# Placing the sample rows' search and ranking in one stretch of VectorE's order, and storing their mask already repeated for 128 partitions

## The chip, the cores and the metric

The kernel runs on one core of a Trainium2 chip. The metric is the device time of one launch in microseconds, and its median over three runs before the change is 3454.47 us (3447.92 to 3465.7). The engines are named as in the profile: PE (TensorE, matrix products and transposes), DVE (VectorE), ACT (ScalarE), POOL (GpSimd) and SP (SyncE), which here does nothing but issue DMAs. Each engine executes its own instructions strictly in the order in which they were written for it.

## The reference: what is computed

One step of a two-layer decoder trunk over 2048 prompt rows and 8 x 4 sample rows, D = 1024. Layer 0 projects the normed rows to two mixers, a sparse attention (A) and a retention (B). For mixer A an indexer gives each row a score for each key, and only the 256 best keys take part in the softmax:

```
sc = where(vis, index_scores(iq, ik, iw), -inf)
_, sel = top_k(sc, 256)            # 256 of 2048 keys for a prompt row, of 2052 for a sample row
ok = sel <= tpos
out = softmax(q . k[sel] where ok) . v[sel]      # GQA, 8 heads over 2 key heads
```

A sample row has 2048 keys in a paged cache and 4 new ones, so 2052 scores. Layer 1 is a gated DeltaNet and is not touched.

## The kernel before

The program is five stages with a barrier between them: `layer0_project`, `layer0_mixers`, `layer0_samples`, `layer0_out_and_conv` and `layer1_delta`. The change touches the second and the third.

In `layer0_mixers` the 2048 prompt rows are 16 tiles of 128 rows. A tile f passes through turning (`turn_q`, `turn_k`, `turn_b`), the retention (`ret_scores`, `ret_mask`, `ret_out`, `ret_update`, `gn_mean`, `gn_square`), the indexer (`index` on PE, `relu` on ACT, `weigh` on DVE), `bounds`, a bisection of 24 steps for the score of rank 256 (`count` on DVE for even tiles, `signs`/`side`/`move` on ACT for odd ones), `rank` and `mask`, and then attention (`scores` on PE, `masked` on DVE, `maxima`, `exp`, `turn_p`, `copy_p`, `times_v`). Beside all this PE computes the second half of the input projection (`project`), two contraction blocks at a time with weights that SP brings into four buffers (`load_w`, 512 KB each), and each load waits until `project` has let its buffer go.

The order in which each engine takes these steps is a list that `mixers_order` makes: each step has a place number (100 for one tile's round), the steps are sorted by it, and each engine walks its own part of the list. Signals (semaphores) only make an engine wait; they never change its order.

The 32 sample rows are searched for their 256 best keys in the same stage, by the steps of `sample_steps`. `s_bounds` gives the interval, `s_count` is one bisection step (one pass of DVE over 32 x 2052 scores and two tiny instructions), 24 of them; `s_rank` resolves ties: a pass for the scores above the interval, one for those within it, a running sum over them (a scan), and three passes that turn it into a mask of 0 and -1e30 in `s_row`. Before the change `s_rank` is cut into four steps that stand at four places with other work between them; `s_store` then writes the mask to `mb_s` in DRAM. The ties lie in the buffer `signs`, and ACT's first use of `signs` for tile 3 waits for the mask.

In `layer0_samples` partition 32 i + 8 r + q of `mb` needs the mask of sample row 8 i + q, for head r of 4, so each mask row is needed four times. SP's list there begins with some thirty loads, `mb` among them, then `gng`, `zb` and `za`; ACT's first instruction of the stage waits for all loads of `zb` and `za`, and everything that ACT copies for PE comes behind it.

Of the kernel before, what the change touches and what calls it, by code (L numbers as in the profile page):

```python
# [16 lines left out]
BF = mybir.dt.bfloat16  # L17
# [6 lines left out]
P = 128  # L24
D = 1024
# [480 lines left out]
def sample_steps(add):  # L506
# [18 lines left out]
    for k in range(STEPS):  # L525
        add(-226 + 10.0 * k if k < 2 else -177 + 7.4 * (k - 2), "dve", "s_count", k)
    for k in range(4):
        add((-8, 13.5, 33.5, 53.5)[k], "dve", "s_rank", k)
    add(90, "sp", "s_store")
# [33 lines left out]
def layer0_mixers(nc, io, S, both):  # L563
    ctx = ExitStack()
    with ctx:
# [15 lines left out]
        overm, signs = sb("overm", [P, SEQ], BF), sb("signs_out", [P, SKEYS], BF)  # L581
# [335 lines left out]
        def _(act):  # L917
# [37 lines left out]
            def count_signs(s, k):  # L955
                W = (s + 1) * P
                if (s, k) == (3, 0):
                    act.wait_ge(S["s_mask_ready"], after(1))
# [109 lines left out]
        def _(dve):  # L1068
            link, fresh = link_in(dve, S["dve_link"])

            def weigh(f, c, j):
# [5 lines left out]
                if j == 0:  # L1077
                    if (f, c) == (4, 0):
                        dve.wait_ge(S["s_mask_stored"], after(16))
# [159 lines left out]
            def s_rank(k):  # L1239
                w = s_halves[:, STEPS - 3:STEPS - 2]  # L1240
                over, tie, more, need_s = above[0:SR, :], signs[0:SR, :], cgt[0:SR], need[0:SR]
                if k == 0:
                    link(dve.tensor_tensor(hi_c[0:SR], s_mid, w, ALU.add))
                    link(dve.tensor_tensor(lo_c[0:SR], s_mid, w, ALU.subtract))
                    link(dve.tensor_scalar(over, s_row, hi_c[0:SR], 0.0, ALU.is_gt, ALU.add, accum_out=more))
                    link(dve.tensor_scalar(need_s, more, -1.0, float(TOPK), ALU.mult, ALU.add))
                elif k == 1:
                    link(dve.scalar_tensor_tensor(tie, s_row, lo_c[0:SR], over, ALU.is_gt, ALU.subtract))
                elif k == 2:
                    link(dve.tensor_tensor_scan(s_row, tie, tie, 0.0, ALU.add, ALU.bypass))  # L1250
                else:
                    link(dve.scalar_tensor_tensor(tie, s_row, need_s, tie, ALU.is_le, ALU.mult))
                    link(dve.tensor_tensor(tie, tie, over, ALU.add))
                    dve.tensor_scalar(s_row, tie, BIG, -BIG, ALU.mult, ALU.add).then_inc(S["s_mask_ready"], 1)
# [3003 lines left out]
```

## Time and profile before

| | |
|---|---|
| median of 3 runs | 3454.47 us (3447.92 to 3465.7) |
| the profiled execution's own time | 3465.7 us |
| its span, first to last instruction | 3464.1 us, so 1.6 us lie around it |
| PE busy | 3156.4 us, 91% |
| DVE / ACT / POOL busy | 53% / 39% / 26% |
| mean granted clock of PE | 0.957 |
| `layer0_mixers` | from about 375 to 1701 us of the span |
| `layer0_samples` | from about 1702 to 1805 us |

Busy shares are means over stages that have different limits. What a moved instruction is worth is to be read from the stretch in which it stands: which engine waits there, for whom, and how long. In the rows below a time in brackets is how long an engine stood before an instruction, and behind the arrow stands who released it. Where a line says x8 and gives a duration, it is the merged run of that many instructions.

### The profile page before, as it was taken

Reading aid. Unit: us, or ns where it says so; the run is one execution under the profiler, and the core shown is the slowest. Engines: PE = TensorE matmul, PEld = TensorE weight load, DVE = VectorE, ACT = ScalarE, POOL = GpSimd, SP = SyncE. Lnnn points to the kernel's source line nnn. Section 1 sums busy time; section 2 is a strip of 40 time slices with the busy share of each in tenths; the row PEclk is TensorE's granted clock in tenths of the full one; section 3 lists DMA queues with packets and bytes.
Section 4 is the critical chain, followed back from the end, with each engine's and each line's share of the span. In section 5 each row is a group of like instructions: output and inputs, shape, how many; then the busy total and the mean of one; then the engine's idle time right before and its main releaser. Section 6 shows DMA issues by size and latency. Waiting matters only on the chain. (4 is left out here: it accounts for less than half of the span.)

```text
span 3464.1 us, 46915 instructions
## 1 busy us (share of the span) xinstructions
PE 3156.4 (91%) x15557; PEld 1725.7 (50%) x15557; DVE 1835.2 (53%) x3700; ACT 1366.0 (39%) x2790; POOL 907.6 (26%) x1776
## 2 busy tenths in 40 slices
PE   8998989989998989888669999999999969989998
PEld 4554444444444444444344444444444456656664
DVE  0000496678878888864231531522513857656663
ACT  2221115667676767676332121121121334443442
POOL 2332333322322221000000000000000467765771
PEclk9999999999999999999879999999999989998999
DMA  6666767555443433301257021121111242234211
GB/s 193 179 197 226 226 212 217 174 166 166 137 132 118 126 113 100 120 22 34 86 211 265 25 70 55 31 67 49 37 64 32 65 155 100 84 98 140 80 62 67
DMA packets 260396, 407.35 MB, mean 118 GB/s; under 512 B 47896, under 2 KB 131138, under 8 KB 258978
## 3 DMA queue, kind: packets, MB, share of 16 engines
q1 hardware_dynamic: 237636, 387.64, 34.5%
q0 software_dynamic: 4096, 8.40, 0.9%
q10 hardware_dynamic: 18432, 8.40, 0.9%
q8 instruction: 125, 2.05, 0.2%
q14 instruction: 107, 0.87, 0.1%
HBM read 324.25 MB, written 103.03 MB: 123 GB/s over the span
## 5 line engine op out<-in xcount | busy, mean ns | idle before, releaser
L2576 PE MATMUL QB<-hT,w_c 128*128 128x512 f32 x1024 | 449.3, 593 | 0.0
L814 PE MATMUL PB<-wb,hT_ahead 128*128 128x512 f32 x832 | 417.2, 628 | 10.5 <-PEq L4165 4.6
L2576 PEld LDWEIGHTS QB<-hT,w_c 128*128 128x128 f32 x1024 | 190.1, 190 | 217.6 <-issue 217.6
L358 PE MATMUL P0A<-w_all,hT 128*128 128x512 f32 (+1 forms) x816 | 269.5, 490 | 2.4 <-issue 2.4
L1007 ACT COPY ptT<-PT 128x512 f32<-128x512 f32 (+3 forms) x320 | 164.0, 519 | 248.1 <-PE PT L825 247.7
L2427 PE MATMUL QA<-arena,hT 128*128 128x512 f32 (+1 forms) x768 | 255.1, 487 | 6.3 <-issue 3.0
L3628 PE MATMUL RPJ<-w_co,oT 128*128 128x512 f32 x544 | 250.0, 609 | 4.2 <-ACT oT L3796 3.2
L963 ACT ACTIVATE signs_out<-isc,mid 128x512 bf16<-128x512 f32 (+6 forms) x168 | 229.5, 1366 | 26.6 <-DVE mid L1107 25.5
L1119 DVE TENSOR_SCALAR_CACHE_REDUCE band<-isc,mid 128x384 bf16<-128x384 f32 (+6 forms) x168 | 236.4, 1407 | 1.3
L814 PEld LDWEIGHTS PB<-wb,hT_ahead 128*128 128x128 f32 x832 | 149.3, 198 | 169.0 <-issue 154.0
L3206 POOL TENSOR_SCALAR stat<-stat 128x1 f32<-128x1 f32 x16 | 3.1, 192 | 814.8 <-POOLq L122 814.8
L802 PE MATMUL PS<-kT,qT 64*128 64x512 f32 (+3 forms) x544 | 155.2, 595 | 57.4 <-DVE mxc L1167 57.0
L825 PE MATMUL PT<-ident,sm 128*128 128x128 f32 x1088 | 179.6, 285 | 30.6 <-ACT sm L997 25.4
L4122 POOL TENSOR_TENSOR arena<-arena 128x60 f32<-128x60 f32 (+24 forms) x465 | 167.2, 360 | 125.8 <-DVE arena L3975 91.7
L825 PEld LDWEIGHTS PT<-ident,sm 128*128 128x128 f32 x1088 | 122.6, 142 | 154.5 <-issue 85.1
L358 PEld LDWEIGHTS P0A<-w_all,hT 128*128 128x128 f32 x816 | 133.7, 192 | 127.0 <-issue 126.8
L2427 PEld LDWEIGHTS QA<-arena,hT 128*128 128x128 f32 x768 | 128.2, 193 | 130.6 <-issue 130.6
L2792 ACT COPY raw<-QB 128x512 f32<-128x512 f32 x64 | 37.5, 586 | 393.2 <-PE QB L2576 393.2
L1167 DVE CUSTOM_DVE_ANT_0 sm<-PS,mb 128x512 f32<-128x512 f32 (+3 forms) x272 | 153.9, 603 | 58.4 <-PE PS L802 58.2
L4125 POOL TENSOR_TENSOR arena<-arena 128x60 f32<-128x60 f32 (+24 forms) x465 | 167.8, 361 | 36.4
L997 ACT ACTIVATE sm<-sm,negm 128x128 f32<-128x128 f32 (+15 forms) x128 | 152.5, 1192 | 56.0 <-DVE negm L1179 27.9
L841 PE MATMUL PO<-ptT,vst 128*64 128x128 f32 x2176 | 155.6, 282 | 17.9 <-ACT ptT L1007 17.9
(541 smaller groups left out, 5332.5 us busy)
## 6 DMA issues: line engine op xcount, KB each, us to landing
wb<-in_w_in_ab SPq DMA_DIRECT2D x272, 512.0 KB, 3.8
out_c_all<-crow SPq DMA_DIRECT2D x256, 64.0 KB, 1.7
pra<-out_pr_all SPq DMA_DIRECT2D x16, 546.0 KB, 4.6
x_rows<-in_x_all SPq DMA_DIRECT2D x17, 512.0 KB, 5.8
out_hT_all<-hT SPq DMA_DIRECT2D x17, 512.0 KB, 3.1
arena<-out_c_all SPq DMA_DIRECT2D x17, 512.0 KB, 5.1
arena<-out_gc_rows SPq DMA_DIRECT2D x17, 512.0 KB, 3.7
cv<-out_c_all SPq DMA_DIRECT2D x17, 512.0 KB, 5.0
```

What stands on the lines that cost most here:

```text
L358: ins = pe.matmul(PA[u % 6][:, 0:b - a], hT[:, t % 3, c, :], w_all[:, c, a:b], start=(c == 0), stop=(c == KD - 1))
L814: ins = pe.matmul(b_bank(g, n)[:, :], h_of(g)[:, 2 * q + k, :], wb[:, u % 4, k, :], start=(q == 0 and k == 0), stop=(q == 3 and k == 1))
L825: ins = pe.transpose(PT[v % 2][:, k * P:(k + 1) * P], sm[:, 2 * (r % 2) + a, c * CH + k * P:c * CH + (k + 1) * P], ident[:, :])
L841: ins = pe.matmul(PO[a * HD:(a + 1) * HD, r * P:(r + 1) * P], vst[:, 4 * c + k, a * HD:(a + 1) * HD], ptT[:, (v + a) % 4, k * P:(k + 1) * ...
L963: act.activation(signs[:, 0:W], isc[:, s % 3, 0:W], ACT.Sign, bias=mid[:, s % 3:s % 3 + 1], scale=1.0, accum_out=cnt[:, s % 3:s % 3 + 1]). ...
L1007: act.copy(ptT[:, v % 4, 0:w], PT[v % 2][:, 0:w]).then_inc(S["p_copied"], 1)
L1119: link(dve.tensor_scalar(band[:, 0:W], isc[:, k, 0:W], m, 0.0, ALU.is_gt, ALU.add, accum_out=above_it))
L2427: ins = pe.matmul(PA[n % 2][:, 0:b - a], h, w_z[:, c, a:b], start=(c == 0), stop=(c == KD - 1))
L2576: ins = pe.matmul(PB[b % 2][:, 0:N], w_c[:, c, b * P:(b + 1) * P], hT[:, c, 0:N], start=(c == 0), stop=(c == KD - 1))
L3628: ins = pe.matmul(PJ[:, :], oT[:, c, :], w_co[:, c, n * 512:(n + 1) * 512], start=(c == 0), stop=(c == KD - 1))
L4122: link(pool.tensor_tensor(xtmp[:, 0:cl, 0:n], T[:, t % 2, j + 1:SB, j].unsqueeze(1).to_broadcast([P, cl, n]), Xs[:, t % 2, 0:cl, j:j + 1]. ...
L4125: ins = pool.tensor_tensor(Xs[:, t % 2, 0:cl, j + 1:SB], Xs[:, t % 2, 0:cl, j + 1:SB], xtmp[:, 0:cl, 0:n], ALU.subtract)
```

## The change

Five things are changed.

1. The 24 `s_count` steps stand at even distances (every 9.0 places from -226) rather than two at -226 and -216 and the rest every 7.4 places from -177.
2. `s_rank` is one step at place -8 rather than four at -8, 13.5, 33.5 and 53.5. It computes the same instructions in the same order. Its ties lie in `band` rather than in `signs`, which shrinks by four elements, and the wait for the mask moves from ACT (tile 3's first `signs`) to DVE (tile 2's first `count`, behind `s_rank` on the same engine).
3. `s_store` becomes four steps at 71, 75, 79 and 83 rather than one at 90, each of which issues four DMAs of 8 rows: 16 DMAs of 64 KB that write each mask row four times, and `mb_s` has 128 rows.
4. The first `weigh` of tile 4, which overwrites the scores, waits for all 16.
5. `layer0_samples` loads `mb` with one DMA of 128 rows rather than four that each repeat 8 rows four times.

```diff
     for k in range(STEPS):
-        add(-226 + 10.0 * k if k < 2 else -177 + 7.4 * (k - 2), "dve", "s_count", k)
-    for k in range(4):
-        add((-8, 13.5, 33.5, 53.5)[k], "dve", "s_rank", k)
-    add(90, "sp", "s_store")
+        add(-226 + 9.0 * k, "dve", "s_count", k)
+    add(-8, "dve", "s_rank")
+    for i in range(HB):
+        add(71 + 4 * i, "sp", "s_store", i)
...
-                if (s, k) == (3, 0):
-                    act.wait_ge(S["s_mask_ready"], after(1))
...
-                        dve.wait_ge(S["s_mask_stored"], after(16))
+                        dve.wait_ge(S["s_mask_stored"], after(16 * 4 * HB))
...
+                if (s, n) == (2, 0):
+                    dve.wait_ge(S["s_mask_ready"], after(1))
...
-            def s_store():
+            def s_store(i):
                 sp.wait_ge(S["s_mask_ready"], after(1))
-                sp.dma_start(io["mb_s"], s_row).then_inc(S["s_mask_stored"], 16)
+                for r in range(4):
+                    sp.dma_start(io["mb_s"][SR * i + 2 * DT * r:SR * i + 2 * DT * (r + 1), :],
+                                 isc[2 * DT * i:2 * DT * (i + 1), 1, :]).then_inc(S["s_mask_stored"], 16)
...
-                             (bsel[:, :], io["bsel"][0:SR, 0:DB]), (dsel[:, :], io["dsel"])):
+                             (bsel[:, :], io["bsel"][0:SR, 0:DB]), (dsel[:, :], io["dsel"]),
+                             (mb[:, :], io["mb_s"])):
                 sp.dma_start(dst, src, allow_slow_non_contiguous=True).then_inc(S["c4_loaded"], 16)
-            for i in range(HB):
-                sp.dma_start(mb[SR * i:SR * (i + 1), :], io["mb_s"][2 * DT * i:2 * DT * (i + 1), :].partition_broadcast(4))\
-                  .then_inc(S["c4_loaded"], 16)
```

DVE around the retention of tile 1, before. `band,cnt<-isc,mid 32x2052` begins one `s_count`; `attm<-PX,rmask_t` is `ret_mask(1)`, `rst` `ret_update(1)`, `gn<-gx` `gn_mean(1)` and `gn<-gq` `gn_square(1)`.

```order
L1235 TENSOR_SCALAR band,cnt<-isc,mid 32x2052
L1236 TENSOR_SCALAR fin<-cnt,halves 32x1
L1237 SCALAR_TENSOR_TENSOR mid<-fin,halves,mid 32x1
L1260 TENSOR_TENSOR attm<-PX,rmask_t 128x256 x2
L1265 SCALAR_TENSOR_TENSOR ga<-ga,prb 128x512
L1267 SCALAR_TENSOR_TENSOR tgb<-tgb,prb 128x512
L1235 TENSOR_SCALAR band,cnt<-isc,mid 32x2052
L1236 TENSOR_SCALAR fin<-cnt,halves 32x1
L1237 SCALAR_TENSOR_TENSOR mid<-fin,halves,mid 32x1
L1277 SCALAR_TENSOR_TENSOR rst<-rst,cdec_t,PX 128x128 x2
L1284 TENSOR_REDUCE gn<-gx 128x4
```

The same engine and place in the changed kernel, from the sixth `s_count` on.

```order
L1235 TENSOR_SCALAR band,cnt<-isc,mid 32x2052
L1236 TENSOR_SCALAR fin<-cnt,halves 32x1
L1237 SCALAR_TENSOR_TENSOR mid<-fin,halves,mid 32x1
L1256 TENSOR_TENSOR attm<-PX,rmask_t 128x256 x2
L1261 SCALAR_TENSOR_TENSOR ga<-ga,prb 128x512
L1263 SCALAR_TENSOR_TENSOR tgb<-tgb,prb 128x512
L1273 SCALAR_TENSOR_TENSOR rst<-rst,cdec_t,PX 128x128 x2
L1235 TENSOR_SCALAR band,cnt<-isc,mid 32x2052
L1236 TENSOR_SCALAR fin<-cnt,halves 32x1
L1237 SCALAR_TENSOR_TENSOR mid<-fin,halves,mid 32x1
L1280 TENSOR_REDUCE gn<-gx 128x4
L1285 TENSOR_REDUCE gn<-gq 128x4
```

Two counts stand ahead of `ret_mask(1)` before, and six in the changed kernel; the counts that stood between its neighbours are gone from there but for one. Sixteen counts stand ahead of `ret_mask(2)` before and 17 now; all 24 stand ahead of `bounds(2)` in both.

DVE behind `bounds(2)`, the rows of the changed kernel. `above`, `band` and `isc` with 32x2052 are `s_rank`; 128x384 are `count` steps of tile 2; `sm,mxc<-PS,mb` is `masked(0, 0, 0)`.

```order
L1244 TENSOR_SCALAR above,fin<-isc,fin 32x2052
L1245 TENSOR_SCALAR fin<-fin 32x1
L1246 SCALAR_TENSOR_TENSOR band<-isc,fin,above 32x2052
L1247 SCALAR_TENSOR_TENSOR isc<-band 32x2052
L1248 SCALAR_TENSOR_TENSOR band<-isc,fin,band 32x2052
L1249 TENSOR_TENSOR band<-band,above 32x2052
L1250 TENSOR_SCALAR isc<-band 32x2052
L1119 TENSOR_SCALAR band,cnt<-isc,mid 128x384
```

Before, the same instructions stood apart: the first pass here, the second behind two `count` steps and ahead of `masked(0, 0, 0)`, the scan ahead of `weigh(3, 0, 0)` and `masked(0, 1, 0)`, the last three ahead of `masked(0, 2, 0)`. So the scan and three passes are moved ahead of `masked(0, 0, 0)` and of `ret_mask(3)` behind it.

SP, the changed kernel, behind the loads of the projection of tile 4.

```order
L1545 DMA out_yab_all<-yb 128x512
L1524 DMA out_mb_s<-isc 8x2052 x16
L1498 DMA wb<-in_w_in_ab 128x2x512 x4
L1549 DMA out_yab_all<-ya 128x512
```

Before, one `out_mb_s<-isc 32x2052` stood there, behind the first of these four loads. The 16 stand ahead of it.

## Rows read from the trace of the kernel before

**Rows 1.** Order of time, DVE, retention of tiles 1 and 2: start, us, instruction, idle before.
```profile
410.99 0.76 DVE L1260 TENSOR_TENSOR attm<-PX,rmask_t 128x256 f32<-128x256 f32 x2 [4.20 <-PE PX L728]
...
452.27 2.34 DVE L1235 TENSOR_SCALAR_CACHE_REDUCE band<-isc,mid 32x2052 bf16<-32x2052 f32 x1
...
455.13 0.76 DVE L1260 TENSOR_TENSOR attm<-PX,rmask_t 128x256 f32<-128x256 f32 x2
...
459.76 0.61 DVE L1277 SCALAR_TENSOR_TENSOR rst<-rst,cdec_t,PX 128x128 f32<-128x128 f32 x2 [2.67 <-PE PX L742]
```
**Rows 2.** Order of time, PE, the same stretch.
```profile
412.63 0.38 PE L740 MATMUL PX<-prb,attm 128*128 128x128 f32 x2
...
455.94 0.79 PE L740 MATMUL PX<-prb,attm 128*128 128x128 f32 x2 [7.15 <-DVE attm L1260]
...
459.51 2.03 PE L814 MATMUL PB<-wb,vst 128*128 128x512 f32 x4
```
**Rows 3.** Stretches of the span: busy us of each engine, clock, DMA share, GB/s.
```profile
450.00:460.00 10.00, 4.06 (x17) 3.91 (x18) 7.11 (x13) 0.24 (x1) 0.00 (x0) 0.66 0.24 89
1716.00:1727.00 11.00, 1.59 (x8) 1.18 (x6) 0.84 (x5) 0.00 (x0) 0.00 (x0) 0.50 0.28 100
```
**Rows 4.** Order of time, DVE, behind `bounds(2)`.
```profile
497.60 0.29 DVE L1167 CUSTOM_DVE_ANT_0 sm<-PS,mb 128x128 f32<-128x128 f32 x1
...
506.50 4.41 DVE L1250 TENSOR_TENSOR_SCAN isc<-signs_out 32x2052 f32<-32x2052 bf16 x1
510.95 1.08 DVE L1083 TENSOR_SCALAR isc<-relu,iwc 128x512 f32<-128x512 f32 x1
...
512.74 0.28 DVE L1167 CUSTOM_DVE_ANT_0 sm<-PS,mb 128x128 f32<-128x128 f32 x1
...
516.30 2.33 DVE L1252 SCALAR_TENSOR_TENSOR signs_out<-isc,fin,signs_out 32x2052 bf16<-32x2052 f32 x1
...
522.99 0.59 DVE L1119 TENSOR_SCALAR_CACHE_REDUCE band<-isc,mid 128x384 bf16<-128x384 f32 x1
```
**Rows 5.** Order of time, PE, the same stretch and the next round's begin.
```profile
497.95 0.70 PE L802 MATMUL PS<-kT,qT 64*128 64x128 f32 x4 [1.09 <-DVE mxc L1167]
499.87 0.49 PE L740 MATMUL PX<-prb,attm 128*128 128x128 f32 x2 [1.22 <-DVE attm L1260]
...
505.33 1.13 PE L713 MATMUL PX<-ikT,iqT 64*128 64x512 f32 x4
...
513.09 0.69 PE L802 MATMUL PS<-kT,qT 64*128 64x128 f32 x4 [2.89 <-DVE mxc L1167]
513.71 3.12 PE L814 MATMUL PB<-wb,hT_ahead 128*128 128x512 f32 x4
...
540.94 1.88 PE L814 MATMUL PB<-wb,vst 128*128 128x512 f32 x4
```
**Rows 6.** Order of time, ACT, `relu(3, 0, 0)`.
```profile
508.68 1.09 ACT L952 ACTIVATE relu<-PX 128x512 f32<-128x512 f32 x2
```
**Rows 7.** Order of time, SP: when it issues which DMA.
```profile
530.65 0.47 SPq L1547 DMA_DIRECT2D out_yab_all<-yb  x1
...
533.31 0.47 SPq L1527 DMA_DIRECT2D out_mb_s<-isc  x1
...
1714.49 2.82 SPq L1761 DMA_DIRECT2D mb_s<-out_mb_s  x4
```
**Rows 8.** DMA issues of 500 to 560 us: count, KB each, us to landing.
```profile
wb<-in_w_in_ab SPq DMA_DIRECT2D x18, 512.0 KB, 3.7
```
**Rows 9.** The loads of `za`: issue ns, first and last start.
```profile
L1772 SPq DMA_DIRECT2D za_s<-out_pr_all x8: 619/622/792, 1721.2 to 1726.1; - x8
```
**Rows 10.** Order of time, ACT, first instruction of `layer0_samples`.
```profile
1731.31 0.31 ACT L1935 ACTIVATE gb_s<-zb_s 128x128 f32<-128x128 f32 x1 [35.48 <-DMA za_s<-out_pr_all]
```
**Rows 11.** DMA issues of 1700 to 1740 us, a small load.
```profile
ident<-in_ident SPq DMA_DIRECT2D x1, 64.0 KB, 3.1
```

More of the change, by code:

```diff
@@ L580, in layer0_mixers @@
         band, above = sb("band", [P, SKEYS], BF), sb("above", [P, SKEYS], BF)
-        overm, signs = sb("overm", [P, SEQ], BF), sb("signs_out", [P, SKEYS], BF)
+        overm, signs = sb("overm", [P, SEQ], BF), sb("signs_out", [P, SEQ], BF)
         qT, iqT, qkbT = sb("qT", [P, 4, 4, P]), sb("iqT", [P, 2, P]), sb("qkbT", [P, 4, P])
@@ L1237, in s_count, with s_rank @@
                 link(dve.scalar_tensor_tensor(s_mid, ph[0:SR], s_halves[:, n + 1:n + 2], s_mid, ALU.subtract, ALU.add))
-            def s_rank(k):
+            def s_rank():
                 w = s_halves[:, STEPS - 3:STEPS - 2]
[L1241 to L1254, printed above, removed]
+                over, tie, more, need_s = above[0:SR, :], band[0:SR, :], cgt[0:SR], need[0:SR]
+                link(dve.tensor_tensor(hi_c[0:SR], s_mid, w, ALU.add))
+                link(dve.tensor_tensor(lo_c[0:SR], s_mid, w, ALU.subtract))
+                link(dve.tensor_scalar(over, s_row, hi_c[0:SR], 0.0, ALU.is_gt, ALU.add, accum_out=more))
+                link(dve.tensor_scalar(need_s, more, -1.0, float(TOPK), ALU.mult, ALU.add))
+                link(dve.scalar_tensor_tensor(tie, s_row, lo_c[0:SR], over, ALU.is_gt, ALU.subtract))
+                link(dve.tensor_tensor_scan(s_row, tie, tie, 0.0, ALU.add, ALU.bypass))
+                link(dve.scalar_tensor_tensor(tie, s_row, need_s, tie, ALU.is_le, ALU.mult))
+                link(dve.tensor_tensor(tie, tie, over, ALU.add))
+                dve.tensor_scalar(s_row, tie, BIG, -BIG, ALU.mult, ALU.add).then_inc(S["s_mask_ready"], 1)
             def ret_mask(f):
@@ L1336, in _ @@
                 elif name == "s_rank":
-                    s_rank(*which)
+                    s_rank()
                 elif name == "o_add":
@@ L1612, in _ @@
                 elif name == "s_store":
-                    s_store()
+                    s_store(*which)
                 else:
@@ L1617, in _ @@
             sp.wait_ge(S["sample_stored"], after(16))
-            sp.wait_ge(S["s_mask_stored"], after(16))
+            sp.wait_ge(S["s_mask_stored"], after(16 * 4 * HB))
             sp.wait_ge(S["ya_stored"], after(16 * NT))
@@ L1670 @@
         "yab_all": (ROWS, D), "y1_all": (ROWS, D), "zg_all": (ROWS, D), "c_all": (ROWS, CC), "pr_all": (ROWS, ABW),
-        "hT_all": (ROWS, D), "mb_s": (SR, SKEYS), "gc_rows": (NT + 1, D),
+        "hT_all": (ROWS, D), "mb_s": (P, SKEYS), "gc_rows": (NT + 1, D),
         "g_idx": (HB, P, NPG, 2, HD), "g_k": (HB, P, NPG, 2, 2, HD), "g_v": (2, P, 8, DB, P)}
-N_CONST4 = 6 + HB + RH
+N_CONST4 = 7 + RH
 def layer0_samples(nc, io, S):
```

## The prediction

> **What bounds the kernel now.** I read the page's busy shares first: PE is busy for most of every stage, so what makes PE stand is what costs time. Then DVE's and PE's instructions in order of time around the sample search (about 401 to 530 us), then SP's list at 530 us, and last the start of `layer0_samples`.
>
> DVE is the engine that ends last in this stretch. One `s_count` takes 455.13 - 452.27 = 2.86 us [rows 1], 24 of them 69 us, and they share DVE with the retention steps on which PE waits. DVE was ahead at tile 1, where it stood 4.20 us before `ret_mask(1)` [rows 1] and PE took `ret_out(1)` at 412.63 without a wait [rows 2]. It was behind at tile 2: PE stood 7.15 us before `ret_out(2)` [rows 2], and DVE had no idle time before `ret_mask(2)` at 455.13 [rows 1]. A stop also costs clock. The stretch of 450 to 460 us had a granted clock of 0.66 [rows 3], so part of it ran at 1.2 GHz, and `ret_out(2)` took 459.51 - 455.94 = 3.57 us [rows 2], of which half, 1.8 us, would be gone at 2.4 GHz.
>
> **Part 1, the counts at even distances.** Before, DVE was free at 410.99 - 4.20 = 406.79. Four more counts stand there now: 4 x 2.86 = 11.4, so `ret_mask(1)` starts at 418.2 rather than 410.99, 7.2 late. PE starts `ret_out` 0.81 us after `ret_mask` (455.94 - 455.13), so at 419.0 rather than 412.63: a new stop of 6.4 us, and 1.8 for the slow clock behind it. PE is 8.2 late.
>
> Between `ret_mask(1)` and `ret_mask(2)` stood 14 counts in 455.13 - 410.99 = 44.1 us; now 11 stand there: 44.1 - 3 x 2.86 = 35.5. But `ret_update(1)` and `gn_square(1)` have lost the count that stood ahead of them and must wait for PE and for POOL. The nearest row is the 2.67 us before `ret_update(2)` [rows 1], where no count stood either; twice that is 5.4. So `ret_mask(2)` starts at 418.2 + 40.9 = 459.1, 4.0 late, and so does `ret_out(2)`. PE reaches it at 448.8 + 8.2 = 457.0 and stands 3 us where it stood 7.15. Of the 8.2 us only 4.0 are left: the new stop mostly takes the place of the old one. From there to `bounds(2)` stand 7 counts rather than 8, so DVE is 4.0 - 2.9 = 1.2 late there.
>
> **Part 2, the ranking in one piece.** The scan (510.95 - 506.50 = 4.45 us) and the three last passes (522.99 - 516.30 = 6.7) [rows 4] move ahead of `masked(0, 0, 0)` at 497.60 and of `ret_mask(3)`. Behind them are queued, on DVE, all the retention steps and all the attention steps of tile 0, and PE waits for two of them with hardly any room: 1.09 us before `scores(0, 1, 0)` and 1.22 us before `ret_out(3)` [rows 5]. Both come 1.2 + 4.45 + 6.7 = 12.3 late. PE, 4.0 late by then, stands about 9.4 us (497.95 - 1.09 + 4.0 = 500.9, to 510.3). `ret_out(3)` was slow only in its second half, so the clock adds 0.8: PE is 13.1 late.
>
> What comes back? PE stood 2.89 us before `scores(0, 2, 0)` at 513.09 [rows 5], which waits for `masked(0, 1, 0)` behind the scan. With the scan gone that wait does not go, because another chain is late next: `index(3, 0, 0)` on PE at 505.33 [rows 5], `relu` on ACT, over at 508.68 + 1.09 = 509.77 [rows 6], `weigh` on DVE, which began at 510.95, `masked` [rows 4]. The scan cost this chain only 510.95 - 509.77 = 1.2. So 13.1 - 1.2 = 11.9 stay. The four `project` products behind that wait took 3.12 us against 1.88 at full clock [rows 5]; with a shorter wait some of these 1.2 us may come back, and I take 0.4. Part 1 and 2 together: +11.5 us on PE. The lower bound is 7: all of the 2.89 (1.7 more), the other 0.8 of the clock, and 2 us because the weight buffers fill while PE stands. The upper is 14: nothing comes back and one more such wait. What replaces the stall is thus not hidden: PE has no slack behind it, and DVE, which catches up within the next round, cannot give PE's time back.
>
> The wait that moved to DVE stands behind `s_rank` on the same engine and costs nothing. ACT's wait for the mask was over long before tile 3's first `signs`, whose bounds come later; nothing is gained. The buffers' names and sizes change no instruction's shape.
>
> **Part 3, 16 stores.** SP's time per store is 0.47 us [rows 7]. The 16 start when the store of `yb` is issued (530.65 + 0.47 = 531.12; with PE late all of this is late alike) and end 7.5 us later, at 538.6. Only then comes the load of the first weights of the next projection, which lands 3.7 us later [rows 8], at 542.3; PE wanted it at 540.94 [rows 5]. Cost 1.4 us. The other loads of that round have more room, and `weigh(4, 0, 0)`, which waits for all 16, lies over 10 us behind. Bounds: 0 if the stores are issued quicker, as `wb` loads are; 4.4 if the stores move at the rate of the worst DMA stretch that I see, 100 GB/s [rows 3]: 1.05 MB in 10.5 us, 3 us longer than their issue, with the load behind them.
>
> **Part 4, one load of `mb`.** In `layer0_samples` ACT's first instruction, and with it all that it copies for PE, stood until the last load of `za` had landed, at 1731.31 [rows 10]; that load was issued at 1726.1 [rows 9]. SP's issues are a chain: the four `mb` loads took 2.82 us [rows 7], and one takes about 0.47. So `za` is issued 2.3 us earlier. Its landing took 1731.31 - 1726.1 = 5.2 us, where a load of 64 KB in the same stage took 3.1 [rows 11]. In between the DMA engines' busy share was only 0.28, 4.5 of 16, at 100 GB/s [rows 3]: 1716 to 1727 us at that rate is 1.1 MB, just the four `mb` loads. If `za` queues behind them on the same few engines, 2 us of its landing go with them. I take 2.3 + 2.0 = -4.3. Bounds: -2.1 (landing as before and an issue of 0.7 us) and -4.5.
>
> The Trainium skill bears on this place (DMA: Bandwidth & Descriptors, "Why a DMA increments its semaphore by 16 and not by 1" and "Rules for kernel authors"). A DMA runs on the largest number of engines, up to 16, that divides the slowest dimension of both its sides, and on the lowest-numbered ones. A fourfold repeat outermost gives four engines, and `za`, whose source has four heads outermost, shares them; the trace's 4.5 busy engines agree, and by that rule the 2.0 us of landing are right. The rule speaks against Part 3: stores of 8 rows run on 8 engines. At the row's 100 / 4.5 = 22 GB/s an engine this is 178 GB/s, 5.9 us, still less than the 7.5 us of issue, so by it the sum stays.
>
> **The sum.** +11.5 + 1.4 - 4.3 = +8.6 us. Against the profiled execution (span 3464.1, 1.6 around it, 3465.7) that gives 3474.3; this execution was the slowest of the three, 11.2 above the median, so the forecast is 3454.5 + 8.6 = 3463. The likeliest case's own range is +2.5 (7 + 0 - 4.5) to +16.3 (14 + 4.4 - 2.1): 3457 to 3471.
>
> **The rivals.**
> A. PE's lateness is swallowed. Up to 1700 us PE has further waits for `masked`; where DVE's ranking holds them rather than PE's own scores, a late PE stands less. For it: place 2 of Part 1 does just that, taking 4.2 of 8.2 us back. Against it: behind 530 us DVE mostly waits for PE and ACT. Price: 0 + 1.4 - 4.3 = -2.9, so 3452.
> B. Slower by more than the measurement: the clock stays down. PE's longest stop in the stretch becomes 9.4 us where it was 7.15. For it: in 1716 to 1727 the clock is 0.50 throughout, with PE hardly working [rows 3]. Against it: behind 7.15 us it came back within about 4 us of work [rows 2]. Its place is 510 to 541 us. From 513.71 to 540.94 PE has 27 us of work; if half of it ran at 1.2 GHz, some 12 us come on top: +20.6, 3475. It decides once slow work behind the stop lasts over about 9 us longer than I count.
> C. The stores back up for longer than their bound, with several of the four weight buffers empty in turn: another 4 us, +12.6, 3467, still within the band.
> D. The reordering does not hold PE, because `ret_mask` and `masked` are not what releases it. Then only the loads count: like A or better, 3450.
>
> **How the numbers follow.** What a measurement of this kernel can tell from no change is 0.5%, 17 us. The forecast has 0.60 (same), A 0.17 (same), B 0.12 (slower), C 0.07 (same, a seventh of it beyond), D 0.04 (a quarter of it scatters to faster). With 0.01 for something unseen on either side: faster 0.02, same 0.84, slower 0.14. The range reaches down to A's 3452 less 4 for scatter, and up to B's 3475: 3448 to 3475.
>
> **What would show it.** Right: six counts end at about 418 and PE stands 6 to 7 us before `ret_out(1)` and about 3 before `ret_out(2)`; PE stands 9 to 10 before `scores(0, 1, 0)`; the first weights of tile 5's projection come 1 to 2 us late; ACT's first instruction of `layer0_samples` starts about 4 us less far into the stage. The mixers' stage is 12 to 13 us longer and the samples' 4 shorter. Wrong: no new stop at tile 1, or a mixers' stage that grows by under 5 us or over 18, or `mb` landing no earlier.

## The result and the profile after

| | before | changed |
| --- | --- | --- |
| median, us | 3465.7 | 3478.0 |
| lowest to highest, us | 3447.9 to 3480.2 | 3468.6 to 3497.3 |
| the profiled execution, us | 3465.7 | 3475.5 |
| its span, us | 3464.1 | 3473.9 |

Over 11 runs of each, changed to before is 1.0051, with a 95% interval of 1.0030 to 1.0073. That is 17.7 us slower, between 10.4 and 25.3 (the two medians alone differ by 12.3). The forecast was +8.6 us and 3463 us. Both of its parts missed: the change costs more than the sum had, and the kernel before, whose three runs had a median of 3454.5, has 3465.7 over eleven.

Where the time went is read at markers that both traces have. One is the transposes of `oT_a` on PE, which end a tile's attention. The first two of each kernel, in order of time, before and then after:

```profile
540.45 0.66 PE L850 MATMUL PO<-ident,oT_a 128*128 128x128 f32 x4 [0.69 <-ACT oT_a L1027]
590.24 0.66 PE L850 MATMUL PO<-ident,oT_a 128*128 128x128 f32 x4 [0.69 <-ACT oT_a L1027]
```
```profile
547.70 0.66 PE L850 MATMUL PO<-ident,oT_a 128*128 128x128 f32 x4 [0.69 <-ACT oT_a L1025]
...
611.89 0.66 PE L850 MATMUL PO<-ident,oT_a 128*128 128x128 f32 x4 [0.69 <-ACT oT_a L1025]
```

Tile 0 is 7.25 us late, which is all that happened before the stores. One trace against one is good to a few us here: tile 0 stands at 538.9 to 544.6 us in the eleven traces with the order of before, and at 547.7 to 548.7 in the four with the new order; the means lie 6.9 apart. From tile 0 to tile 1 it took 64.2 us where it took 49.8: 14.4 more. That is the stretch of the stores, and this distance hardly scatters: it is 49.8 in all ten traces whose mixers' stage has only the one store of before at that place. The samples' stage, from SP's first issue in it, starts 20.45 us later (1722.19 against 1701.74) and hands over to the next stage 4.2 us earlier in itself (109.4 us in, 113.6 before). So 7.25 + 14.4 - 4.2 = +17.5, which agrees with the ratio. The single span shows +9.8 only, since the rest of that execution was some 8 us quicker, 1.2 of it before the samples' stage and 6.4 behind it, where the code is the same. I put that down to scatter: e5 and e13 below have the mixers' stage of before unchanged up to its last tile, and the transposes of that tile stand at 1708.0 us in the one and at 1690.3 in the other.

**The order on DVE.** PE at the three places of Parts 1 and 2, in order of time; [rows 2, 5] are its counterparts.

```profile
460.96 0.49 PE L740 MATMUL PX<-prb,attm 128*128 128x128 f32 x2 [0.86 <-DVE attm L1256]
...
508.06 1.00 PE L802 MATMUL PS<-kT,qT 64*128 64x128 f32 x4 [8.90 <-DVE mxc L1167]
...
521.46 0.70 PE L802 MATMUL PS<-kT,qT 64*128 64x128 f32 x4 [1.14 <-DVE mxc L1167]
```

Ahead of `ret_out(1)`, at 419.97 us, stands a new stop of 6.63 us. On DVE the sixth count ended and `ret_mask(1)` followed at 419.16 us, against 410.99 [rows 1]. The stop of 7.15 before `ret_out(2)` is down to 0.86, the one of 1.09 before `scores(0, 1, 0)` up to 8.90, and that of 2.89 before `scores(0, 2, 0)` down to 1.14.

DVE reaches `bounds(2)` at 487.82 us, where it was 488.07 before, so it isn't late there. Then come the scan and the passes that were moved forward, and the next `count`; DVE in order of time:

```profile
495.15 5.42 DVE L1247 TENSOR_TENSOR_SCAN isc<-band 32x2052 f32<-32x2052 bf16 x1
...
502.98 1.22 DVE L1249 TENSOR_TENSOR band<-band,above 32x2052 bf16<-32x2052 bf16 x1
504.23 1.22 DVE L1250 TENSOR_SCALAR isc<-band 32x2052 f32<-32x2052 bf16 x1
505.48 0.61 DVE L1119 TENSOR_SCALAR_CACHE_REDUCE band<-isc,mid 128x384 bf16<-128x384 f32 x1
```

They take 505.48 - 495.15 = 10.3 us, not 4.45 + 6.7 = 11.15. The scan is 1 us slower than before. The last two passes took 2.18 us each before, with POOL at work beside them without a gap, and take 1.22 here, with POOL idle; e5 again has 2.18 with POOL at work, e1 and e7 have 1.22 with POOL idle. That POOL makes the difference was not tested by itself: the buffer of the ties differs as well.

**The stores.** SP in order of time around them; `out_mb_s<-isc x16` are the 16 stores.

```profile
537.90 0.47 SPq L1545 DMA_DIRECT2D out_yab_all<-yb  x1
538.41 16.13 SPq L1524 DMA_DIRECT2D out_mb_s<-isc  x16
554.59 3.50 SPq L1498 DMA_DIRECT2D wb<-in_w_in_ab  x4
```

The stores' line, with ns of the shortest, the median and the longest:

```profile
L1524 SPq DMA_DIRECT2D out_mb_s<-isc x16: 297/1072/1429, 538.4 to 553.3; - x16
```

PE, waiting for the weights behind them:

```profile
560.40 3.75 PE L814 MATMUL PB<-wb,vst 128*128 128x512 f32 x4 [12.04 <-DMA wb<-in_w_in_ab]
```

Stretches there, with us and count busy of PE, PEld, DVE, ACT and POOL, then clock, DMA share (the mean busy share of the 16 DMA engines) and GB/s:

```profile
544.00:549.00 5.00, 3.67 (x18) 1.63 (x16) 0.61 (x2) 2.63 (x7) 0.00 (x0) 1.00 0.40 59
549.00:553.00 4.00, 0.00 (x0) 0.00 (x0) 3.75 (x17) 0.10 (x1) 0.00 (x0) 0.76 0.47 60
554.00:555.00 1.00, 0.00 (x0) 0.00 (x0) 0.00 (x0) 0.00 (x0) 0.00 (x0) 0.50 0.63 66
555.00:556.00 1.00, 0.00 (x0) 0.00 (x0) 0.00 (x0) 0.00 (x0) 0.00 (x0) 0.50 0.56 57
```
```profile
562.00:564.00 2.00, 2.00 (x4) 0.57 (x3) 0.00 (x0) 0.00 (x0) 0.00 (x0) 0.50 1.03 374
564.00:566.00 2.00, 2.00 (x14) 1.47 (x13) 0.00 (x0) 0.03 (x1) 0.00 (x0) 0.83 0.95 247
```

The DMA engines are half busy and move 60 GB/s, as slow with every other engine idle (66 and 57 GB/s from 554 to 556 us) as beside their work. The first weights are issued at 554.59 us and release PE 5.8 us later, not 3.7 [rows 8]. PE stands 12.04 us, works at 1.2 GHz until about 565, and pays 1.9 us on the first four products alone (3.75 against 1.88 [rows 5]); from tile 0 to tile 1 it is busy 48.9 us rather than 46.6. 12.0 and the 2.3 of this clock make the 14.4.

**The load.** SP and ACT in the samples' stage, in order of time, against [rows 7, 9, 10]:

```profile
1736.02 0.43 SPq L1758 DMA_DIRECT2D mb_s<-out_mb_s  x1
```
```profile
L1768 SPq DMA_DIRECT2D za_s<-out_pr_all x8: 620/620/755, 1740.2 to 1745.0; - x8
```
```profile
1747.10 0.31 ACT L1931 ACTIVATE gb_s<-zb_s 128x128 f32<-128x128 f32 x1 [30.74 <-DMA za_s<-out_pr_all]
```

ACT starts 24.91 us into the stage where it started at 29.57: 4.66 earlier. The last `za` load is issued 22.8 us in rather than 24.4, and lands in 2.1 us rather than 5.2. PE's stop for ACT fell from 14.92 to 10.02 us.

### The profile page after: what moved, and what is told of

The parts are those of the page before. It is cut to its first block and busy times, and to the rows that moved or that the text cites. A ratio compares the mean times of both kernels' runs of the same rounds, so it can differ in the third digit from the quotient of the medians.

```text
span 3473.9 us, 46925 instructions
## 1 busy us (share of the span) xinstructions
PE 3147.0 (91%) x15557; PEld 1719.3 (49%) x15557; DVE 1829.7 (53%) x3700; ACT 1366.7 (39%) x2790; POOL 897.9 (26%) x1776
```

## The experiments

"tile 0 to 1" below is the distance of the two transposes above (49.8 us before, 64.2 changed); "into the stage" counts from SP's first issue in `layer0_samples`. Both are read from one trace of each kernel; ratios to before are of launch times, with their 95% interval.

### The order alone: e1_order

The changed kernel's counts and ranking, with the one store and the four loads of before.

```diff
-    for i in range(HB):
-        add(71 + 4 * i, "sp", "s_store", i)
+    add(90, "sp", "s_store")
```

> The changed kernel with the store and the load of the mask as before: only DVE's order and the buffer of the ties are changed. Theory (the two causes add): the mixers' stage is 7 us longer than before by the transpose of tile 0's output, with stops of 6.6 us before ret_out(1) and 9 us before scores(0, 1, 0), and no stop for weights at 548 us; 7 us stay to the end of the stage. Rival (the order is free, the 16 stores are all of it): under 3 us, because PE's later waits swallow it. Rival (a shift of 7 grows later): over 12 us at the end of the stage.

1.0031 of before, 1.0018 to 1.0045 (3470.4 against 3461.7 us). Tile 0 at 547.7 us, 7.25 late as in the changed kernel, tile 0 to 1 49.8, and the samples' stage begins 7.3 us late. The stops stand where Parts 1 and 2 had them; PE in order of time:

```profile
417.02 0.79 PE L739 MATMUL PX<-prb,attm 128*128 128x128 f32 x2 [6.61 <-DVE attm L1255]
...
459.04 0.53 PE L739 MATMUL PX<-prb,attm 128*128 128x128 f32 x2 [3.71 <-DVE attm L1255]
...
507.59 1.00 PE L801 MATMUL PS<-kT,qT 64*128 64x128 f32 x4 [9.04 <-DVE mxc L1166]
```

So PE's lateness is not swallowed (rival A): the ratio is +10.7 us, 6.2 to 15.6, and the trace has at the end of the stage what stood at tile 0. That it doesn't grow either rests on the one trace, which scatters by more than this.

### The stores alone: e2_stores

The kernel before, with the 16 stores in place of the one.

```diff
-    add(90, "sp", "s_store")
+    for i in range(HB):
+        add(71 + 4 * i, "sp", "s_store", i)
```

> The kernel before with only the 16 stores of 8 rows; the load still repeats 8 rows four times. Theory: SP needs 16 us for them rather than 7.5, and PE stands 12 us for the first weights of tile 5's projection; the stage is about 14.5 us longer (12 and 2 to 2.5 for the slow clock behind the stop). Rival (the stop came only because DVE's order had made PE late): SP takes 7.5 us and PE stands under 3.

1.0056 of before, 1.0039 to 1.0073 (3479.6 against 3461.7), which is 13.5 to 25.3 us. Tile 0 is on time, tile 0 to 1 takes 63.7 us (+14.0). SP again, in order of time:

```profile
531.35 15.10 SPq L1529 DMA_DIRECT2D out_mb_s<-isc  x16
546.50 2.60 SPq L1503 DMA_DIRECT2D wb<-in_w_in_ab  x2
```

PE stood 10.92 us for `wb`. In the traces order and stores add up: 7.3 + 14.0 = 21.3 in these two, 7.25 + 14.4 in the change. The stores cost twice what the order does.

### The same bytes in four stores: e3_four32

```diff
-                for r in range(4):
-                    sp.dma_start(io["mb_s"][SR * i + 2 * DT * r:SR * i + 2 * DT * (r + 1), :],
-                                 isc[2 * DT * i:2 * DT * (i + 1), 1, :]).then_inc(S["s_mask_stored"], 16)
+                sp.dma_start(io["mb_s"][SR * i:SR * (i + 1), :], s_row).then_inc(S["s_mask_stored"], 16)
```

The difference is shown against e2_stores; the 32 rows go out four times, and the four loads of before read the first 32 rows of `mb_s`, as ever.

> As the one with 16 stores, but the same 1.05 MB go in 4 stores of 32 rows at the same places. Theory E (each DMA engine moves one row of 8208 bytes in about 1 us, and an 8-row store uses 8 engines): 32 rows on 16 engines take 2 us a store, so SP is held for at most 8 us and PE stands 0 to 4 us. Theory I (SP needs 1 us to issue any such store): SP takes 4 us, PE does not stand. Theory P (it is the 8 partitions that are slow to read): 4 stores in 4 us or less in all. Theory B (the bytes are the limit, at 65 GB/s): again 16 us and a stop of 12.

One run. The four took SP 3.58 us and landed 5.3 us after their issue; PE's stop for `wb` was 0.71 us; tile 0 to 1 took 54.0. It is not the number of bytes: by that landing time the last of the same 1.05 MB was out some 8 us after the first issue (theory B is refuted; E, I and P all allow this). Of the 4.2 us over 49.8 the stop is 0.7, and 3.5 are PE's work at a lower clock (busy 50.1 us rather than 46.6, clock 0.94 rather than 1.00); why the clock fell in this trace is not shown.

### The stores apart: e7_apart

The changed kernel with one store every 3.7 places of the order, rather than four together.

```diff
-        add(71 + 4 * i, "sp", "s_store", i)
+        for r in range(4):
+            add(71 + 3.7 * (4 * i + r), "sp", "s_store", i, r)
```

> The changed kernel with its 16 stores one by one between the weight loads, 3.7 places apart from 71 to 127. Theories E and P (the engines are what is slow, SP is only held back when stores queue up): each store takes SP 0.3 to 0.5 us, no stop over 2 us for weights, so the mixers' stage is 12 to 14 us shorter than in the changed kernel. Theory I: each takes SP about 1 us also when it stands alone. Rival (the lowest 8 engines delay every weight load by their 1 us): many small stops for weights, 5 to 10 us in sum.

1.0011 of before, 0.9994 to 1.0028, below the whole interval of the changed kernel. The median issue is 389 ns, tile 0 to 1 takes 52.6 us, 11.6 less than in the changed kernel, and PE's longest stop for `wb` there is 0.8. (The samples' stage begins only 5.6 us earlier than in the changed kernel's trace, not 12 to 14; see the scatter above.) Where weight loads stand between them the stores are quick; the first five, which still stand in a row, took 4.41 us, 0.9 each. What is slow is one behind another.

### What makes a row of stores slow: e9_rows_alone, e10_row_length, e11_same_rows, e13_ports

Four kernels add stores to the one before at the end of the mixers' stage, where every engine is idle, in groups that SP waits for. First the number of rows and their places, from `kT`, 512 KB a group:

```diff
+            for rows, step in ((8, 1), (8, 16), (16, 1), (32, 1), (64, 1)):
```

> The kernel before, with added stores at the end of the mixers' stage, when the DMA engines are idle: 512 KB of kT in rows of 8192 bytes go to a scratch tensor in five groups, each waited for before the next: 8 stores of 8 neighbouring partitions, 8 stores of 8 partitions that lie 16 apart, 4 stores of 16, 2 of 32 and one of 64. It times the stores by themselves. Theory E (a store of 8 rows takes 8 engines, one row each, and a row takes an engine about 1 us): both groups of 8 rows take 7 to 9 us from first issue to last landing beside the fixed 2 us, the stores of 16 rows about half of that, 32 and 64 the same half. Theory P (neighbouring partitions share a way out of the memory): the neighbouring 8 take 7 to 9 us, the 8 that lie 16 apart 4 us or less. Theory L (the odd length of 8208 bytes makes rows slow): every group takes 4 us or less.

From a group's first issue to the next group's it took 6.1 us for 8 neighbouring rows (the 6.8 that the next run's text gives is wrong), 6.7 for rows 16 apart, 4.3 for stores of 16 and 3.9 for stores of 32. In the groups of 8 rows eight engines or fewer were busy (share 0.42 at 127 GB/s from 1697 to 1699 us, neighbours; 0.43 at 109 GB/s from 1703 to 1706, 16 apart). Stores of 16 and 32 rows are quicker (shares of 0.57 and 0.66), as theory E has it, but its 1 us a row is not there: at 127 GB/s each of 8 engines has some 0.5 us for a row of 8192 bytes. P in this first form fell, as both groups of 8 were nearly alike. Next the length and the spacing:

```diff
+            for name, length in (("scr_a", SKEYS), ("scr_b", SEQ), ("scr_c", SKEYS), ("scr_d", SEQ)):
```

> The run before this one stored rows of 8192 bytes on idle DMA engines: 8 stores of 8 rows took 6.8 us with their landing, at 125 to 131 GB/s on 8 engines, an engine's row in 0.5 us, where the changed kernel's stores ran at 62 to 66 GB/s, a row in 1.0 us. So the eight engines are confirmed and the 1 us is not. This is the kernel before with stores at the end of the mixers' stage again, five groups of 8 stores of 8 rows, each group waited for: (a) rows of the mask tile, 8208 bytes into a tensor whose rows lie 8208 bytes apart, as the change stores them; (b) 8192 bytes into the same spacing; (c) 8208 bytes into rows 8256 bytes apart; (d) 8192 into rows 8192 apart; (e) kT's rows again, 8192 into 8192. Theory L (a row that isn't a whole number of 512-byte pieces, or starts off such a boundary, takes twice as long): (a) takes 9 to 11 us, (d) and (e) 6 to 7; (b) against (c) tells whether the length or the spacing does it. Theory C (what slowed the stores in the changed kernel was what else ran then: other traffic and engines that read the same memory): all five groups take 6 to 7 us.

Theory L is refuted. SP, in order of time, the five groups:

```profile
1702.50 3.86 SPq L1624 DMA_DIRECT2D out_scr_a<-isc  x8
1708.64 3.85 SPq L1624 DMA_DIRECT2D out_scr_b<-isc  x8
1714.77 4.01 SPq L1624 DMA_DIRECT2D out_scr_c<-isc  x8
1721.07 3.84 SPq L1624 DMA_DIRECT2D out_scr_d<-isc  x8
1727.19 3.78 SPq L1629 DMA_DIRECT2D out_scr_e<-kT  x8
```

All five are alike and quick, 6.1 to 6.3 us from one to the next. In these groups no two neighbouring stores read the same partitions. The change's do, four in a row:

```diff
+            for name, order in (("scr_a", [(i, r) for i in range(4) for r in range(4)]),
+                                ("scr_b", [(i, r) for r in range(4) for i in range(4)])):
```

> The run before this one refuted theory L: groups of 8 stores took 6.1 us each for every length and spacing. And the trace of the changed kernel speaks against theory C too: in 553 to 556 us TensorE, VectorE, ScalarE and GpSimd are all idle there, and the stores still run at 57 to 66 GB/s. Two differences are left: the change issues 16 in a row and not 8, and its four neighbours in a row read the same 8 partitions. This is the kernel before with three groups of 16 stores of 8 rows at the end of the mixers' stage, engines idle, each group waited for: (a) the order of the change, four times the same 8 partitions and then the next 8; (b) the same 16 stores with the 8 partitions changing from each store to the next; (c) 16 stores of kT's rows, each from 8 partitions of its own. Theory S (two stores of the same partitions at once halve each other): (a) takes 14 to 18 us for its issues, (b) and (c) 8 us. Theory W (after some 5 to 8 stores in a row the writes back up, whatever they read): all three take 13 to 18 us. Theory M (it needs the traffic of the mixers' stage behind it): all three take 8 us.

Theory S. SP in order of time, and two stretches with clock, DMA share and GB/s last:

```profile
1697.30 14.37 SPq L1626 DMA_DIRECT2D out_scr_a<-isc  x16
1715.83 7.69 SPq L1626 DMA_DIRECT2D out_scr_b<-isc  x16
1726.35 8.11 SPq L1631 DMA_DIRECT2D out_scr_e<-kT  x16
```
```profile
1698.00:1712.00 14.00, 0.00 (x0) 0.00 (x0) 0.00 (x0) 0.00 (x0) 0.00 (x0) 0.50 0.50 65
1716.00:1724.00 8.00, 0.00 (x0) 0.00 (x0) 0.00 (x0) 0.00 (x0) 0.00 (x0) 0.50 0.41 109
```

The same 16 stores, in the change's order, take 14.4 us and run at 65 GB/s, and in the other order 7.7 us. Engines idle or not, that is the 60 GB/s of the changed kernel. Theories W and M are refuted. Whether it is the partition or something that several partitions share, the last of the four asks:

```diff
+            for name, firsts, step in (("scr_a", (0,), 1), ("scr_b", (0, 32), 1), ("scr_c", (0, 8), 1),
+                                       ("scr_d", (0, 64), 1), ("scr_e", (0,), 4)):
```

> The run before showed that 16 stores of 8 rows take 14.4 us where four in a row read the same 8 partitions, and 7.7 to 8.1 where the partitions change. This is the kernel before with five groups of 16 stores of 8 rows of kT (8192 bytes, 1.05 MB a group) at the end of the mixers' stage, engines idle, each group waited for: (a) partitions 0 to 7, 16 times; (b) 0 to 7 and 32 to 39 in turn; (c) 0 to 7 and 8 to 15; (d) 0 to 7 and 64 to 71; (e) the 8 partitions 0, 4, 8 to 28, 16 times. Theory S (stores of the same partitions hold each other up): (a) and (e) take 14 to 18 us for their issues, (b), (c) and (d) 7 to 9. Theory P (what is shared is a way out of the memory that several partitions use, here that of neighbours by fours): (a) takes 14 to 18 us, (e) 7 to 9, and of (b), (c) and (d) those are quick whose two sets lie on different ways. By the Trainium skill (SBUF — State Buffer, "Door 1: The DMA port swizzle") partitions in fours share a port and +32 stays on the same one, so 0 to 7 and 32 to 39 are the same two ports of 16: by it (b) is as slow as (a) and (c) and (d) are quick.

SP in order of time:

```profile
1693.83 17.94 SPq L1627 DMA_DIRECT2D out_scr_a<-kT  x16
1715.72 17.60 SPq L1627 DMA_DIRECT2D out_scr_b<-kT  x16
1737.42 9.45 SPq L1627 DMA_DIRECT2D out_scr_c<-kT  x16
1749.29 9.60 SPq L1627 DMA_DIRECT2D out_scr_d<-kT  x16
1761.12 11.16 SPq L1627 DMA_DIRECT2D out_scr_e<-kT  x16
```
```profile
1695.00:1711.00 16.00, 0.00 (x0) 0.00 (x0) 0.00 (x0) 0.00 (x0) 0.00 (x0) 0.50 0.48 50
1717.00:1733.00 16.00, 0.00 (x0) 0.00 (x0) 0.00 (x0) 0.00 (x0) 0.00 (x0) 0.50 0.48 50
1738.00:1746.00 8.00, 0.00 (x0) 0.00 (x0) 0.00 (x0) 0.00 (x0) 0.00 (x0) 0.50 0.49 96
```

Alternating with partitions 32 to 39 helps nothing (b, 17.6 us, 50 GB/s); alternating with 8 to 15 or 64 to 71 doubles the rate (c and d, 96 and 102 GB/s). Theory S is refuted in its narrow form, P holds: what is full is a path that partitions 0 to 7 and 32 to 39 share. All five groups write to DRAM in the same way, so it isn't the target; the targets had changed along with the partitions in e11. Group (e) reads the same 8 partitions 16 times, but spread in fours; it moves 93 GB/s (1762 to 1772 us) and ends 1.2 us behind its last issue, against 3.9 for (a), so nothing is queued up there. Its 11.2 us are SP's time to issue rows that aren't neighbours, about 0.7 us a store, more than the 7 to 9 us expected. The change's order moves on to other partitions after four stores, which is why I take its 60 to 65 GB/s to lie above the 50 of (a).

The Trainium skill (SBUF — State Buffer, "Door 1: The DMA port swizzle") says just this: four neighbouring partitions share one of 16 ports, and 32 further on lies the same one. Eight neighbouring rows are then two ports. The trace agrees: 50 GB/s is 25 GB/s for each of two, where the page's figure for all 16 (about 435 GB/s) makes 27 a port.

### The changed kernel with another order of its stores: e12_other_order

```diff
-                for r in range(4):
-                    sp.dma_start(io["mb_s"][SR * i + 2 * DT * r:SR * i + 2 * DT * (r + 1), :],
-                                 isc[2 * DT * i:2 * DT * (i + 1), 1, :]).then_inc(S["s_mask_stored"], 16)
+                for j in range(HB):
+                    sp.dma_start(io["mb_s"][SR * j + 2 * DT * i:SR * j + 2 * DT * (i + 1), :],
+                                 isc[2 * DT * j:2 * DT * (j + 1), 1, :]).then_inc(S["s_mask_stored"], 16)
```

> The changed kernel with its 16 stores in another order: the 8 partitions that a store reads change from one to the next, nothing else. Theory S: SyncE issues the 16 in 7 to 9 us, TensorE's stop of 12.0 us for wb falls under 5, tile 1's transposes come 50 to 57 us behind tile 0's (64.2 in the changed kernel), and the launch is 6 to 12 us shorter than the changed kernel's (0.9995 to 1.003 of before). Theories W and M: nothing changes, 15 to 16 us for the 16, a stop of 10 to 13, 62 to 65 us, and 1.004 to 1.006 of before.

SP and PE in order of time, and the stretch behind the stop:

```profile
539.10 8.96 SPq L1524 DMA_DIRECT2D out_mb_s<-isc  x16
548.10 1.01 SPq L1498 DMA_DIRECT2D wb<-in_w_in_ab  x2
```
```profile
552.89 3.75 PE L814 MATMUL PB<-wb,vst 128*128 128x512 f32 x4 [3.86 <-DMA wb<-in_w_in_ab]
```
```profile
552.00:558.00 6.00, 5.11 (x11) 2.44 (x12) 1.62 (x8) 0.00 (x0) 0.00 (x0) 0.50 1.00 309
```

1.0028 of before, 0.9998 to 1.0059. Two loops exchanged bring the 16 stores from 16.1 us to 9.0, PE's stop from 12.0 to 3.9 and tile 0 to 1 from 64.2 to 56.7 us. The gain is shown in this stretch; in the launch it is not, since the interval overlaps that of the changed kernel, 1.0030 to 1.0073. The 6.9 that are left over 49.8 are the stop and 5 to 6 us of work at 1.2 GHz behind it, which costs its half.

### The gain without the stores: e4_repeat_late, e5_mask_behind, e6_tanh_behind, e8_repeat_tanh

The samples' term was worth 4 us. Can it be had without its price? First the repeat, made late in the mixers' stage by four copies from DRAM to DRAM:

```diff
+    for r in range(4):
+        add(1400 + 0.1 * r, "sp", "s_repeat", r)
...
+                             (mb[:, :], io["mb_4"])):
```

> The kernel before, its order and its one store untouched; four DMAs from DRAM to DRAM repeat the mask late in the mixers' stage (place 1400, where the DMA engines are nearly idle), and the next stage loads it with one DMA as in the changed kernel. Theory: the mixers' stage is as before within 1.5 us, the samples' stage is 4.6 us shorter (ACT starts 24.9 us behind the first load's issue rather than 29.6), -4 to -5 in all. Rival (the gain in the samples' stage needs nothing but the shorter list of SP): -2.3.

0.9993 of before, 0.9973 to 1.0012. ACT starts 26.24 us into the stage, not 24.9, as two other loads' issues took 2.5 us more than before; the next stage starts 2.8 us earlier, 110.8 us in. No cost shows in the mixers' stage (tile 0 to 1: 49.8). Second, the four slow loads put behind the keys' second load:

```diff
+            for i in range(HB):
+                sp.dma_start(mb[SR * i:SR * (i + 1), :], io["mb_s"][2 * DT * i:2 * DT * (i + 1), :].partition_broadcast(4))\
+                  .then_inc(S["mb4_loaded"], 16)
             for i in range(2, HB):
```

> The kernel before with its four repeating loads of the mask moved behind the second load of keys, and a signal of their own. Theory (ACT is held by za, which stands behind the four slow loads on SP and on the engines): ACT starts 4.6 to 5 us earlier, the samples' stage is 4.5 us shorter, as with the single load. Rival (the four loads on few engines delay the second keys instead): PE waits for keys, and 0 to 3 us are gained.

1.0001, 0.9980 to 1.0022: ACT starts 3.8 us earlier, but the next stage starts 113.3 us in, 0.4 earlier than before. The rival was right: PE now waits 2.2 us for keys and 2.5 for values. Third, that and ACT's tanh, which waits for `za`, behind its first 8 copies of the keys:

```diff
+                if u == 8:
+                    act.wait_ge(S["z4_loaded"], after(16 * (RH + 2 * HB)))
+                    act.activation(gb[:, :], zb[:, :], ACT.Tanh, scale=0.5)
```

> The same, and ACT's two tanh of the gates, which alone need zb and za, stand behind its first eight copies of keys. Theory: PE's stop of 14.9 us before the second group of key transposes goes; late next are the constants of c4 (gng), which now land at about 1722 rather than 1729, so the samples' stage is 10 to 14 us shorter than before and the launch faster by 0.3 to 0.4%. Rival (the clock of 0.5 in this stretch stays and the state loads are late next): 5 to 8 us.

0.9993, 0.9973 to 1.0013. The next stage starts 111.7 us in, 2.0 earlier than before, where 10 to 14 were expected. PE's stop for ACT is gone and one for the keys is in its place; PE in order of time:

```profile
1732.87 6.59 PE L1822 MATMUL ST<-ident,rows_b 128*128 128x128 f32 x32 [1.61 <-DMA rows_b<-out_g_k]
...
1756.18 6.03 PE L1822 MATMUL ST<-ident,rows_b 128*128 128x128 f32 x28 [11.92 <-DMA rows_b<-out_g_k]
```

The fourfold loads now stand ahead of the third load of the keys on SP, and I took it that they hold it up. Then both edits are needed together, the quick load and the moved tanh. This kernel is e4_repeat_late with the `u == 8` lines above:

> The kernel before, with the packed masks of the samples' stage repeated fourfold in DRAM by four copies at place 1400 of the mixers' stage and loaded by one instruction, and ScalarE's tanh of the decoder's part of that stage put behind its first 8 key copies. My theory: both causes found apart add up. The masks' load lands in about 5 us, so nothing holds back keys_in(2); TensorE's stop for ScalarE (14.9 us before) goes, and no stop of more than 3 us for a DMA takes its place; from the first issue of the stage to TensorE's first instruction of the next one it is 103 us or less where it was 113.6, and the launch is 8 to 12 us shorter (0.9965 to 0.9977 of before). Rival L: what is late next is a load (keys or values) whose issue stands behind others on SyncE; then the stage is shorter by 3 to 5 us only, and TensorE shows a stop of over 3 us for a DMA. Rival N: the stage's end is set by VectorE or ScalarE in its second half; the stops move but the stage is within 3 us of what the repeat alone gave (110.8).

0.9952 of before, 0.9935 to 0.9968 (3448.2 against 3464.9 us), the one version that beats both kernels. The next stage starts 101.1 us into this one, 12.5 earlier than before. ACT copies keys from the start, and PE's only stop for a DMA is short; ACT, then PE:

```profile
1720.60 1.16 ACT L1952 COPY kT<-ST 128x512 f32<-128x512 f32 x2 [0.17 <-PE ST L1830]
1725.29 0.31 ACT L1947 ACTIVATE gb_s<-zb_s 128x128 f32<-128x128 f32 x1 [3.54 <-DMA za_s<-out_pr_all]
```
```profile
1732.25 3.38 PE L1830 MATMUL ST<-ident,rows_b 128*128 128x128 f32 x16 [2.82 <-DMA rows_b<-out_g_k]
```

Rivals L and N are refuted, and the stop of 11.9 us for the keys went with the fourfold loads. The launch gained 16.6 us by the ratio, 11.1 to 22.5, where 8 to 12 were expected; the 12.5 of this stage lie within that interval.

## Why the prediction was wrong

**Part 3, the stores, is the step that failed.** It took "SP's time per store is 0.47 us", from a store that stood alone and had 32 rows or more [rows 7]. The 16 took 1.01 us each (16.13 / 16), 8.6 us more in all. As a mechanism the part named the right wait: the stores are issued, and only then the load of the weights for which PE stands. It gave the stop 1.4 us, and it was 12.0: the 1.4, the 8.6, and 2.1 because the weights, queued behind the stores, came 5.8 us after their issue and not 3.7. With the clock behind it the term is +14.4. The bound of 4.4 was too small as well. It took 100 GB/s, from a stretch of loads [rows 3], for the worst rate. The stores ran at 60. e11, e12 and e13 show why: eight neighbouring rows leave by a way that carries 50 GB/s, and four stores in a row use the same one. The part also left out the clock behind its own stop, which Parts 1 and 2 did count: in e12, where the stores are nearly as quick as forecast (9.0 us against 7.5), the stretch still costs 6.9 us.

The prediction's check by the number of engines had 22 GB/s for each, 178 GB/s on eight. Eight engines it was: the share is 0.50 in e11 and 0.48 in e13. But the engines were not what was full; each of the eight moved 60 / 8 = 7.5 GB/s.

Rival C was near to this, stores that back up, at the wrong size: "another 4 us", with a chance of 0.07. The case ended beyond it, at +17.5 rather than +12.6, and its several empty buffers did not show: from tile 0 to tile 1 PE had the one stop for weights.

**Parts 1 and 2 were right in mechanism and over half too large.** They gave +7.25 us at tile 0 against +11.5, at the lower bound of 7 within the scatter of this place. The stop at tile 1 was forecast 6.4 and was 6.63, and the two waits behind it that the part guessed at 5.4 were 2.67 and 2.60; `ret_out(2)` comes 5.0 late and not 4.0, with a stop of 0.86 where 3 were forecast in this execution and 3.71 in e1. The first thing mis-sized is how late `scores(0, 1, 0)` comes, 508.06 - 497.95 = 10.1 and not 12.3: DVE was to be 1.2 late at `bounds(2)` and was 0.25 early (its wait before `ret_update(2)`, for one, fell from 2.67 to 0.94), and the ranking took 10.3 rather than 11.15. The second is what comes back: of the 10.1 us, `scores(0, 2, 0)` still has 8.4 and tile 0's end 7.25. The forecast let 1.2 of 13.1 come back, then 0.4. The lower bound had named sources for this (the 2.89, the clock, the buffers); how the 2.9 that came back divide among them was not worked out.

**Part 4 was right.** -4.66 us at ACT against -4.3. Its halves were 1.6 for the issues (2.3 forecast, as the loads ahead of them took 1 us more) and 3.1 for the landing (2.0 forecast). It arrives at the next stage as -4.2.

**The rivals.** A is refuted by e1, whose launch is 6.2 to 15.6 us longer with nothing but the order changed. B, a clock that stays down after the longest DVE stop, did not occur: the four `project` products behind `scores(0, 1, 0)` at 513.63 took 1.88 us, full clock. D fell with the new stop at tile 1. The time came out above the range by none of the four, but by Part 3's own wait.

**The base.** The ratio's +17.7 stands on a median of 3465.7. With its own +8.6 on that the forecast would have said 3474.3, and the range from 3459 to 3486 would have held the 3478. The other way round, the measured +17.7 on the 3454.5 gives 3472, inside the range as it stood, but only because that reached up to B's 3475, and B's clock did not occur: a hit would have been luck. So the miss of the range is in part the base: three runs whose median lay 11 us under that of eleven. The miss of the change itself, +8.6 against 10.4 to 25.3, is Part 3.

## What to carry to other kernels

Ask of a store or load of few rows not only how many engines it gets but which partitions it touches, and whether its neighbours in the queue touch the same: here exchanging two loops brought the 16 issues from 16.1 us to 9.0. A queue's time per issue, taken from one that stands alone, was only a lower bound; behind slow transfers the issuing engine was held, and what was queued behind them, here the weights, was late by the whole difference. And where a stage waits for several things at one point, removing one shows the next: e4, e5 and e6 gained nothing that could be measured, and e8, which takes two away together, gained 12.5 us in its stage and 0.48% of the launch.

## What the runs showed of the hardware

- Stores from 8 neighbouring partitions, the same 8 each time, ran at 50 GB/s, the same with 32 to 39 in turn, and 96 to 102 GB/s with 8 to 15 or 64 to 71 in turn (e13).
- SP is held while such stores are queued: 0.28 to 0.30 us for the first, 0.98 to 1.24 as the median of 16 (e11, the changed kernel, e13).
- A store of 8 rows that lie 4 apart took SP 0.63 us to issue, the quickest of 16 as well as the median (e13), and rows 16 apart 0.56 to 0.65 (e9), where the first of a row of stores of neighbours took 0.28 (e13).
- The length of a row (8192 or 8208 bytes) and the spacing of its targets (8192, 8208, 8256) made no difference: 3.8 to 4.0 us for 8 stores (e10).
- After 12 us of standing still PE worked at 1.2 GHz until about 565 us, some 4 us of work; after 3.9 us of it in e12 the clock was 0.50 as well, until 558.
- Two DVE passes over 32 x 2052 bf16 took 2.18 us each with POOL at work beside them (before, e5) and 1.22 with POOL idle (the changed kernel, e1, e7).
